# Two transformer blocks on one core: single steps between the matmul passes put together in twos

## The chip, the cores and the metric

The kernel runs on one core of one Trainium2 chip. The metric is the device time of one execution, in microseconds (us). Before the change the median of three runs is 1921.94 us (1920.91 to 1922.42).

The engines' names in the profile: PE is TensorE (its weight loads are a row of their own, PEld), DVE is VectorE, ACT is ScalarE, POOL is GpSimd, SP issues most transfers. Each engine works through its own queue in order, and semaphores hold an instruction until what it needs is there.

## The reference, cut to what matters

Two blocks follow each other on x of 512 tokens by 1024. In the first: a modulated norm, stick-breaking attention of 16 heads, a retention of 4 heads, gates, an output projection and an FFN. In the second: an attention over chosen keys of 8 heads, a gated linear attention, a projection and an FFN.

```python
# block 1
proj = einsum('bsd,de->bse', hmix, w_in[l])
z = einsum('bhtd,bhsd->bhts', qb, kb) * scale            # stick breaking, block of 128 queries
log_1m_beta = where(mask, log_sigmoid(-z), 0.0)
after = cumsum(log_1m_beta, axis=3, reverse=True) - log_1m_beta
a = where(mask, exp(log_sigmoid(z) + after), 0.0)
outs.append(einsum('bhts,bhsd->bhtd', a, vb))
...
scores = einsum('bhncd,bhnmd->bhncm', qc, kc) * decay_mask   # retention
intra = einsum('bhncm,bhnme->bhnce', scores, vc)
...
x = x + gate1 * einsum('bsd,de->bse', merged, w_out[l])
...
# block 2
logits = einsum('bqhd,bqkhd->bqhk', qb, kg) * A_HEAD_DIM ** -0.5 + bias
p = softmax(where(valid, logits, NEG), axis=-1)
o_a = einsum('bqhk,bqkhd->bqhd', p, vg)
...
return rmsnorm_2(x, norm_final)
```

## The kernel before

Nearly all of TensorE's time goes to large products. Each weight tile is split into a high and a low part (`wh`, `wl`: ACT copies the high part from `stg`, POOL or DVE subtracts to get the low part), each activation likewise, and one **pass step** of a job is three matmuls of 128x128 weights with 512 columns: high by high, low by high, high by low (L1465, L1466, L1468). Eight such steps make one job, one output tile of 128 features by 512 tokens. POOL's subtraction for a weight tile is L2559.

Between pass steps stands the other work of PE: products in plain fp32 and transposes. It comes from Python generators. A planner writes one list of steps, in which every engine finds its own in that order. After each pass step `slot` adds the stage's rate to a credit and advances the first generator in `p.fore` by one `yield` for each whole credit. So a `yield` in a generator is a place where pass steps may come in between, `rest(m)` is m of them, and what two yields enclose stands on PE with nothing between. `p.later` holds steps that are emitted after a following job. `take` and `give` hand out the eight PSUM banks from rings: G (three banks, the jobs), Z and C (two each), O (one). `take` only decides the order; that a bank has been emptied is waited for on the chip (`free`).

The generators that the change touches:

- `attend(pr)`, one for each of eight pairs of heads, at rate 1.3. Scores come in three groups (`sbz`, L1511); DVE adds the mask (L1808); ACT takes two sigmoids (`sba`, L2261 and L2263); DVE runs the product scan over one and multiplies the other with it (`sbr`, L1819 and L1823), which gives five tiles of weights `zs`; PE turns each by four 128x128 transposes (`sbt`, L1495 `bank<-ident,zs`); ACT copies the turned tile out (`sbe`, L2269); `sbo` (L1531) multiplies with the values.
- `v_after(pr)`: the values of a pair are turned (`sbvt`, L1495) one job after their product is done.
- `retain(hh)`: three score products (`rs`, L1547) and four products with the values (`rvv`, L1561), one to a yield.
- `out_job(f)`: the turn of an x tile (`x2t`, L1588) stands ahead of each output job.
- `attn()`: 16 items (pair, block of queries). Item n has its logits (`al`, L1689, 64 rows of the array for each of two heads), the maximum (`ag`), the exponential (`ae`), the division (`as`, L2112), the turned weights (`at`, L1697), their copies by ACT (`ac`, L2492) and the values (`av`, L1710, 64 columns of the array for each of two heads). Logits of item n, turns of item n-2 and values of item n-3 stand in three different slots of an iteration.
- `turn_x()`: the final turns of x (`xo`, L1495 `bank<-ident,XR`), one in every eight slots.

Of the kernel before, what the change touches and what calls it, by code (L numbers as in the profile page):

```python
# [16 lines left out]
KT = D // P  # L17
# [232 lines left out]
def make_plan():  # L250
    p = Plan()
# [109 lines left out]
    def attend(pr):  # L361
        if pr == 0:
            emit("tables", "sb")

        def scores(g):
            for hh in range(2):
                take("Z", ("sbz", pr, g, hh))
            emit("sbz", pr, g)
            for hh in range(2):
                give(("sbz", pr, g, hh))  # L370

        def turned(n):
            take("C", ("sbt", pr, n))
            emit("sbt", pr, n)
            yield
            emit("sbe", pr, n)
            give(("sbt", pr, n))

        scores(0)
        yield from rest(3)  # L380
        emit("sba", pr, 1)
        yield from rest(2)
        emit("sba", pr, 2)
        scores(1)
        yield from rest(2)
        emit("sbr", pr, 1)
        yield from rest(2)
        emit("sba", pr, 0)
        yield
        emit("sbr", pr, 2)  # L390
        yield
        scores(2)
        yield from turned(1)
        yield
        emit("sbr", pr, 0)
        emit("sba", pr, 3)
        yield from rest(2)
        yield from turned(2)
        yield
        emit("sba", pr, 4)  # L400
        yield
        emit("sbr", pr, 3)
        yield from turned(0)
        yield from rest(2)
        emit("sbr", pr, 4)
        yield from rest(2)
        yield from turned(3)
        yield from rest(3)
        yield from turned(4)
        yield from rest(2)  # L410
        while ("v", pr) not in p.known:
            yield
        take("O", ("sbo", pr))
        emit("sbo", pr)
        yield
        yield
        p.split("os", pr, "pool")
        emit("sbw", pr)
        give(("sbo", pr))
        yield  # L420

    def v_after(pr):
        def turn():
            take("G", ("sbvt", pr))
            emit("sbvt", pr)
            give(("sbvt", pr))
            p.known.add(("v", pr))
        p.later.append([1, turn])
        p.fore.append(attend(pr))

    for p2 in range(1, 4):
# [50 lines left out]
        emit("factor", key)  # L482

    def retain(hh):
        for n in range(3):
            take("Z", ("rs", hh, n))
            emit("rs", hh, n)
            give(("rs", hh, n))
            yield
        while ("rv", hh, 3) not in p.known:  # L490
            yield
        for d in range(4):
            take("C", ("rvv", hh, d))
            emit("rvv", hh, d)
            give(("rvv", hh, d))
            yield
        yield
        yield
        take("O", ("r", hh))
# [99 lines left out]

    def out_job(f):  # L600
        def fn(n):
            take("Z", ("x2t", f))
            emit("x2t", f)
            give(("x2t", f))
            take("G", ("gemm", n, 0), 0)
            p.gemm(n)
            p.of["out", f] = n
# [342 lines left out]
    def attn():  # L950
# [31 lines left out]
        for n in range(len(ITEMS) + 3):  # L982
            if wanted(n, 0):
                logits(n)
            if wanted(n, 1):
                emit("ae", n - 1)
            yield
# [13 lines left out]
            if n < 3:  # L1001
                yield
                yield
            if wanted(n, 3):
                while ("VA", ITEMS[n - 3][0]) not in p.known:
                    yield
                values(n - 3)
            if wanted(n, 1):
                emit("as", n - 1)
            yield  # L1010
# [47 lines left out]
    def turn_x():  # L1058
# [4 lines left out]
        factor("n4")  # L1063
        give("n4")
        p.known.add("r4")
        for k in range(KT):
            for _ in range(8):
                yield
            take("Z", ("xo", k))
            emit("xo", k)  # L1070
            give(("xo", k))

    def norm4():
        p.mark("last")
# [1614 lines left out]
```

## Time and profile before

| | us |
|---|---|
| median of 3 runs | 1921.94 |
| lowest, highest | 1920.91, 1922.42 |
| the profiled execution | 1923.94 |
| its span, first to last instruction | 1922.1 |
| PE busy in the span | 1879.3 |
| DVE, ACT, POOL busy | 868.0, 687.2, 516.4 |

The profiled execution lies 2.0 us above the median of the runs, and 1.8 us of it lie outside the span. Matmuls are pipelined: a row's length reaches into the next one, so a cost on PE is read from the starts of rows. A bracket at the end of a row gives the idle time ahead of it and who ended it.

### The profile page before, as it was taken

What the parts mean: (1) busy time and instruction counts of PE and PEld (TensorE: products, weight loads), DVE (VectorE), ACT (ScalarE), POOL (GpSimd) and SP (SyncE); (2) the same over time, 40 slices, a digit from 0 to 9 for tenths busy, and PEclk for the clock granted to TensorE, in tenths of its full rate; (3) what the DMA queues carried; (4) which work ended last, traced back from release to release, by engine and by line L of the source; (5) the groups of instructions that cost most, each with busy time, mean ns of one, the idle gap of its engine ahead of it and who ended that gap; (6) DMA issues with size and microseconds to landing.
All of it is one profiled execution on the core that took longest, in us unless ns stands there. A gap on an engine that the chain in (4) does not pass through costs nothing.

```text
span 1922.1 us, 21539 instructions
## 1 busy us (share of the span) xinstructions
PE 1879.3 (98%) x8653; PEld 1463.2 (76%) x8653; DVE 868.0 (45%) x1352; ACT 687.2 (36%) x1021; POOL 516.4 (27%) x285
## 2 busy tenths in 40 slices
PE   7999999999999999989999999999999999999998
PEld 6777778878777777867888888777676778888886
DVE  6466542645261213334333333657477654423433
ACT  5555541223232323443221223425446432212223
POOL 4433334444353534410000000234345311100100
PEclk9999999999999999999999999999899999999999
DMA  9411223534443223324323322422122123222321
GB/s 302 144 46 65 66 66 132 175 121 153 132 141 100 66 88 110 102 74 118 114 82 95 108 80 77 113 88 84 58 72 73 46 99 104 93 88 89 108 88 44
DMA packets 182332, 192.47 MB, mean 100 GB/s; under 512 B 10155, under 2 KB 166065, under 8 KB 181977
## 3 DMA queue, kind: packets, MB, share of 16 engines
q1 hardware_dynamic: 179704, 180.84, 29.3%
q0 software_dynamic: 1104, 5.24, 1.0%
q10 hardware_dynamic: 1424, 5.00, 0.7%
q8 instruction: 70, 1.15, 0.3%
q14 instruction: 30, 0.24, 0.0%
HBM read 188.95 MB, written 4.72 MB: 101 GB/s over the span
## 4 chain that ended last, share of the span: by engine, by line
PE 87%; DVE 8%; ACT 2%; issue 2%; POOL 1%; DMA 0%; ACTq 0%; DVEq 0%; SPq 0%; POOLq 0%
PE bank L1465 23%; PE bank L1468 23%; PE bank L1466 23%; PE bank L1487 2%; PE bank L1486 2%; PE bank L1485 2%; PE bank L1561 2%; DVE left L1819 2%; PE bank L1495 1%; DVE ADA L1777 1%; PE bank L1531 1%; PE bank L1547 1%; PE bank L1511 1%; PE bank L1447 1%; PE bank L1448 1%
## 5 line engine op out<-in xcount | busy, mean ns | idle before, releaser
L2559 POOL TENSOR_TENSOR wl<-stg,wh 128x1024 fp32r<-128x1024 f32 x150 | 364.8, 2433 | 853.5 <-ACT wh L2200 853.1
L1465 PE MATMUL bank<-hH,wh 128*128 128x512 f32 x1264 | 522.6, 413 | 6.3 <-DVE hL L1933 6.0
L1468 PE MATMUL bank<-hH,wl 128*128 128x512 f32 x1264 | 502.4, 397 | 0.0
L1466 PE MATMUL bank<-hL,wh 128*128 128x512 f32 x1264 | 502.1, 397 | 0.0
L2200 ACT ACTIVATE wh<-stg 128x1024 fp32r<-128x1024 f32 (+2 forms) x292 | 298.3, 1024 | 283.6 <-PE bank L1468 202.8
L1465 PEld LDWEIGHTS bank<-hH,wh 128*128 128x128 f32 x1264 | 239.2, 189 | 78.4 <-issue 25.5
L1468 PEld LDWEIGHTS bank<-hH,wl 128*128 128x128 f32 x1264 | 238.9, 189 | 57.9
L1466 PEld LDWEIGHTS bank<-hL,wh 128*128 128x128 f32 x1264 | 239.8, 190 | 53.5 <-issue 2.9
L1759 DVE TENSOR_TENSOR wl<-stg,wh 128x1024 fp32r<-128x1024 f32 (+2 forms) x142 | 168.4, 1188 | 243.7 <-ACT wh L2200 243.2
L1465 PE MATMUL bank<-h2H,wh 128*128 128x512 f32 x352 | 140.6, 399 | 0.0
L1468 PE MATMUL bank<-h2H,wl 128*128 128x512 f32 x352 | 139.5, 396 | 0.0
L1466 PE MATMUL bank<-h2L,wh 128*128 128x512 f32 x352 | 139.5, 396 | 0.0
L2607 POOL TENSOR_TENSOR tmp<-tmp,SQ 128x512 f32<-128x512 f32 x22 | 28.5, 1294 | 295.6 <-ACT tmp L2388 295.6
L1777 DVE SCALAR_TENSOR_TENSOR ADA<-stg,small,ADA 128x256 f32<-128x256 f32 x112 | 88.7, 792 | 3.7
L1468 PEld LDWEIGHTS bank<-h2H,wl 128*128 128x128 f32 x352 | 66.3, 188 | 16.1
L1466 PEld LDWEIGHTS bank<-h2L,wh 128*128 128x128 f32 x352 | 66.3, 188 | 16.0 <-issue 0.2
L1465 PEld LDWEIGHTS bank<-h2H,wh 128*128 128x128 f32 x352 | 66.3, 188 | 16.0 <-issue 0.2
L1950 DVE TENSOR_TENSOR tmp<-bank,tmp 128x512 f32<-128x512 f32 x44 | 30.4, 692 | 91.6 <-PE bank L1468 91.5
L1468 PE MATMUL bank<-fHa,wl 128*128 128x512 f32 x176 | 69.8, 396 | 0.0
L1465 PE MATMUL bank<-fHa,wh 128*128 128x512 f32 x176 | 69.8, 396 | 0.0
L1466 PE MATMUL bank<-fLa,wh 128*128 128x512 f32 x176 | 69.8, 396 | 0.0
L1819 DVE TENSOR_TENSOR_SCAN left<-tmp,masks 128x384 f32<-128x384 f32 (+2 forms) x64 | 61.9, 999 | 0.0
(324 smaller groups left out, 2565.3 us busy)
## 6 DMA issues: line engine op xcount, KB each, us to landing
stg<-in_w_in SPq DMA_DIRECT2D x54, 1024.0 KB, 5.2
stg<-in_w_ffn_in SPq DMA_DIRECT2D x22, 1024.0 KB, 5.1
stg<-in_w_ada SPq DMA_DIRECT2D x16, 1024.0 KB, 5.2
stg<-in_w_ffn_gate SPq DMA_DIRECT2D x11, 1024.0 KB, 5.1
stg<-in_w_ffn_up SPq DMA_DIRECT2D x11, 1024.0 KB, 5.1
stg<-in_w_ffn_down SPq DMA_DIRECT2D x10, 1024.0 KB, 5.0
stg<-in_w_ada SPq DMA_DIRECT2D x16, 512.0 KB, 6.8
stg<-in_w_proj_ret SPq DMA_DIRECT2D x8, 1024.0 KB, 5.0
```

The costliest lines, as they stand in the source:

```text
L1465: T.matmul(ps, wh, xh, start=j["first"] and k == 0, stop=False)
L1466: T.matmul(ps, wh, xl, start=False, stop=False)
L1468: t = T.matmul(ps, wl, xh, start=False, stop=j["stop"] and last)
L1485: T.matmul(gb[:, :], xh, wh, start=s0, stop=False)
L1486: T.matmul(gb[:, :], xh, wl, start=False, stop=False)
L1487: t = T.matmul(gb[:, :], xl, wh, start=False, stop=s1)
L1561: t = T.matmul(cb[:, j * P:S], v[:, j, d * P:(d + 1) * P], TMP[4 + n][:, off:off + w], start=j == 0, stop=j == 3)
L1759: V.tensor_tensor(lo, src, hi, ALU.subtract).then_inc(s["w_lo_dve"], 1)
L1777: V.scalar_tensor_tensor(last, view[:, k, :], cact[:, k:k + 1], acc, ALU.mult, ALU.add).then_inc(s["ada"], 1)
L1819: t = V.tensor_tensor_scan(left[:, back], tt[:, back], masks[:, 3, back], 1.0, ALU.mult, ALU.add)
L2200: A_.activation(hi, src, ACTF.Copy).then_inc(s["w_hi"], 1)
L2559: G.tensor_tensor(lo, src, hi, ALU.subtract).then_inc(s["w_lo_pool"], 1)
```

## The change

Steps that stood alone between pass steps stand together: the turned weights of the first attention as (1, 2), (0, 3) and (4); the turned values of two pairs; the retention's scores as (0, 1) and (2), its products with the values as (0, 1) and (2, 3); two turns of x ahead of every second output job; two final turns of x after sixteen slots. In the second attention the values of item n-3 move from the third slot of an iteration into the first, behind the logits of item n. Sizes, buffers and the arithmetic stay.

```diff
-        def turned(n):
-            take("C", ("sbt", pr, n))
-            emit("sbt", pr, n)
-            yield
-            emit("sbe", pr, n)
-            give(("sbt", pr, n))
+        def turn(*ns):
+            for n in ns:
+                take("C", ("sbt", pr, n))
+                emit("sbt", pr, n)
+
+        def turned(*ns):
+            for n in ns:
+                emit("sbe", pr, n)
+                give(("sbt", pr, n))
...
         scores(2)
-        yield from turned(1)
+        yield from rest(2)
+        turn(1, 2)
         yield
+        turned(1, 2)
         emit("sbr", pr, 0)
+        yield from rest(2)
         emit("sba", pr, 3)
         yield from rest(2)
-        yield from turned(2)
-        yield
         emit("sba", pr, 4)
         yield
         emit("sbr", pr, 3)
-        yield from turned(0)
-        yield from rest(2)
+        yield from rest(3)
+        turn(0, 3)
+        yield
+        turned(0, 3)
         emit("sbr", pr, 4)
-        yield from rest(2)
-        yield from turned(3)
         yield from rest(3)
-        yield from turned(4)
+        turn(4)
+        yield
+        turned(4)
...
         def turn():
-            take("G", ("sbvt", pr))
-            emit("sbvt", pr)
-            give(("sbvt", pr))
-            p.known.add(("v", pr))
-        p.later.append([1, turn])
+            for q in (pr - 1, pr):
+                take("G", ("sbvt", q))
+                emit("sbvt", q)
+            for q in (pr - 1, pr):
+                give(("sbvt", q))
+                p.known.add(("v", q))
+        if pr % 2:
+            p.later.append([1, turn])
...
-        for n in range(3):
-            take("Z", ("rs", hh, n))
-            emit("rs", hh, n)
-            give(("rs", hh, n))
-            yield
+        for lot in ((0, 1), (2,)):
+            for n in lot:
+                take("Z", ("rs", hh, n))
+                emit("rs", hh, n)
+            for n in lot:
+                give(("rs", hh, n))
+                yield
...
-            take("Z", ("x2t", f))
-            emit("x2t", f)
-            give(("x2t", f))
+            if f % 2 == 0:
+                for g in (f, f + 1):
+                    take("Z", ("x2t", g))
+                    emit("x2t", g)
+                    give(("x2t", g))
...
             if wanted(n, 0):
                 logits(n)
+            if wanted(n, 3):
+                while ("VA", ITEMS[n - 3][0]) not in p.known:
+                    yield
+                values(n - 3)
             if wanted(n, 1):
                 emit("ae", n - 1)
...
-            if wanted(n, 3):
-                while ("VA", ITEMS[n - 3][0]) not in p.known:
-                    yield
-                values(n - 3)
...
-        for k in range(KT):
-            for _ in range(8):
-                yield
-            take("Z", ("xo", k))
-            emit("xo", k)
-            give(("xo", k))
+        for k in range(0, KT, 2):
+            yield from rest(16)
+            for g in (k, k + 1):
+                take("Z", ("xo", g))
+                emit("xo", g)
+                give(("xo", g))
```

The products `rvv` are put together like `rs`, in `((0, 1), (2, 3))`. Lines of the changed file lie 15 lower from L1103 on (L1465 is L1480 there).

PE in the second attention, before: logits of one item (`KA,QA`), then turned weights (`ident,lg`, 8 transposes), then values (`tmp,VA`), a pass step between each:

```order
L1689 MATMUL bank<-KA,QA 128x256 x2
L1465 MATMUL bank<-goH,wh 128x512
L1466 MATMUL bank<-goL,wh 128x512
L1468 MATMUL bank<-goH,wl 128x512
L1697 MATMUL bank<-ident,lg 128x128 x8
L1465 MATMUL bank<-goH,wh 128x512
L1466 MATMUL bank<-goL,wh 128x512
L1468 MATMUL bank<-goH,wl 128x512
L1710 MATMUL bank<-tmp,VA 64x128 x6
```

The same item now:

```order
L1704 MATMUL bank<-KA,QA 128x256 x2
L1725 MATMUL bank<-tmp,VA 64x128 x6
L1480 MATMUL bank<-goH,wh 128x512
L1481 MATMUL bank<-goL,wh 128x512
L1483 MATMUL bank<-goH,wl 128x512
L1712 MATMUL bank<-ident,lg 128x128 x8
```

The values have come up behind the logits, and no pass step stands between the two; the turned weights keep a pass step on either side.

PE in the first attention, third pair of heads, before: the third group of scores (`k2,q2`) and the first turn (`zs1`); four pass steps follow before `zs2`:

```order
L1511 MATMUL bank4<-k2,q2 128x512
L1511 MATMUL bank3<-k2,q2 128x512
L1495 MATMUL bank5<-ident,zs1 128x128 x4
L1465 MATMUL bank1<-hH,wh0 128x512
L1466 MATMUL bank1<-hL,wh0 128x512
L1468 MATMUL bank1<-hH,wl0 128x512
```

The same place now:

```order
L1526 MATMUL bank4<-k2,q2 128x512
L1526 MATMUL bank3<-k2,q2 128x512
L1480 MATMUL bank1<-hH,wh0 128x512
L1481 MATMUL bank1<-hL,wh0 128x512
L1483 MATMUL bank1<-hH,wl0 128x512
L1510 MATMUL bank5<-ident,zs1 128x128 x4
L1510 MATMUL bank6<-ident,zs2 128x128 x4
```

One pass step now parts the scores from the turns (two in some pairs), and the turn of `zs2` has moved up by three pass steps.

ACT in the same pair, before: sigmoids (L2261, L2263) and copies of turned weights (`at1`, `at2`):

```order
L2269 ACTIVATE at1<-bank5 128x512
L2261 ACTIVATE tmp1<-zs3 128x512
L2263 ACTIVATE zs3<-zs3 128x512
L2269 ACTIVATE at2<-bank6 128x512
L2238 ACTIVATE q2<-bank1 128x512
```

ACT there now:

```order
L2284 ACTIVATE at1<-bank5 128x512
L2284 ACTIVATE at2<-bank6 128x512
L2276 ACTIVATE tmp1<-zs3 128x512
L2278 ACTIVATE zs3<-zs3 128x512
L2276 ACTIVATE tmp2<-zs4 128x512
```

The copy of `at2`, which waits for the turn of `zs2`, now stands ahead of the sigmoids of `zs3`.

## Rows read from the trace of the kernel before

**Rows 1.** The page: busy time of each engine, share of the span, instructions.
```profile
PE 1879.3 (98%) x8653; PEld 1463.2 (76%) x8653; DVE 868.0 (45%) x1352; ACT 687.2 (36%) x1021; POOL 516.4 (27%) x285
```

**Rows 2.** Waits of PE: who waited for whom; total, times, longest.
```profile
PE bank L1495 <- DVE zs L1823: 5.0, 8, 1.0
PE bank L1672 <- DVE tmp L2077: 2.1, 1, 2.1
```

**Rows 3.** Timeline of PE, unbroken passes: start, length, what.
```profile
299.70 0.40 PE L1465 MATMUL bank<-osH,wh 128*128 128x512 f32 x1
...
311.89 0.40 PE L1466 MATMUL bank<-osL,wh 128*128 128x512 f32 x1
```

**Rows 4.** Timeline of PE, one turn of weights between passes.
```profile
217.05 0.39 PE L1468 MATMUL bank<-hH,wl 128*128 128x512 f32 x1
217.29 0.60 PE L1495 MATMUL bank<-ident,zs 128*128 128x128 f32 x4
...
218.42 0.39 PE L1465 MATMUL bank<-hH,wh 128*128 128x512 f32 x1
```

**Rows 5.** Timeline of PE, second attention: values, logits, turned weights, values.
```profile
1487.13 0.40 PE L1468 MATMUL bank<-goH,wl 128*128 128x512 f32 x1
1487.46 0.66 PE L1710 MATMUL bank<-tmp,VA 128*64 128x128 f32 x8
...
1488.61 0.40 PE L1468 MATMUL bank<-goH,wl 128*128 128x512 f32 x1
...
1489.57 0.50 PE L1465 MATMUL bank<-goH,wh 128*128 128x512 f32 x1
1489.91 0.39 PE L1466 MATMUL bank<-goL,wh 128*128 128x512 f32 x1
1490.14 0.39 PE L1468 MATMUL bank<-goH,wl 128*128 128x512 f32 x1
1490.37 0.60 PE L1697 MATMUL bank<-ident,lg 128*128 128x128 f32 x4
1490.81 0.60 PE L1697 MATMUL bank<-ident,KI 128*128 128x128 f32 x4
...
1491.71 0.40 PE L1468 MATMUL bank<-goH,wl 128*128 128x512 f32 x1
1492.04 0.88 PE L1710 MATMUL bank<-tmp,VA 128*64 128x128 f32 x12
...
1493.41 0.40 PE L1468 MATMUL bank<-goH,wl 128*128 128x512 f32 x1
```

**Rows 6.** Timeline of PE, third group of scores: third pair, then sixth pair.
```profile
125.29 1.13 PE L1511 MATMUL bank<-k,q 64*128 64x512 f32 x4
...
208.13 1.13 PE L1511 MATMUL bank<-k,q 64*128 64x512 f32 x4
```

**Rows 7.** Timeline of DVE, third pair: products giving zs2 and zs3.
```profile
128.56 0.69 DVE L1823 TENSOR_TENSOR zs<-zs,left 128x511 f32<-128x511 f32 x1
...
133.52 2.88 DVE L1823 TENSOR_TENSOR zs<-zs,left 128x511 f32<-128x511 f32 x1
```

**Rows 8.** Timeline of POOL there: the low part of a weight tile.
```profile
133.44 2.40 POOL L2559 TENSOR_TENSOR wl<-stg,wh 128x1024 fp32r<-128x1024 f32 x1 [7.97 <-ACT wh L2200]
```

**Rows 9.** Timeline of DVE, sixth pair: products giving zs2 and zs3.
```profile
208.41 0.69 DVE L1823 TENSOR_TENSOR zs<-zs,left 128x511 f32<-128x511 f32 x1
...
214.59 0.69 DVE L1823 TENSOR_TENSOR zs<-zs,left 128x511 f32<-128x511 f32 x1
```

**Rows 10.** Timeline of PE, second attention: turn of the first values.
```profile
1442.25 0.66 PE L1495 MATMUL bank<-ident,tmp 128*128 128x128 f32 x4
```

**Rows 11.** Timeline of ACT there: copies of those values.
```profile
1442.94 1.14 ACT L2422 ACTIVATE VA<-bank,small 128x128 f32<-128x128 f32 x4 [0.53 <-PE bank L1495]
```

**Rows 12.** Stretches: length, busy PE, PEld, DVE, ACT, POOL, PEclk, DMA share, GB/s.
```profile
60.00:280.00 220.00, 214.96 (x1264) 160.41 (x1263) 133.54 (x168) 118.15 (x183) 77.57 (x35) 1.00 0.20 64
...
1356.00:1370.00 14.00, 14.00 (x40) 9.50 (x40) 2.89 (x3) 4.88 (x7) 0.84 (x1) 0.52 0.24 76
```

More of the change, by code:

```diff
@@ L484, in retain @@
     def retain(hh):
-        for n in range(3):
-            take("Z", ("rs", hh, n))
-            emit("rs", hh, n)
-            give(("rs", hh, n))
-            yield
+        for lot in ((0, 1), (2,)):
[5 more added lines that the diff above has]
+                yield
         while ("rv", hh, 3) not in p.known:
             yield
[L492 to L495, printed above, removed]
-            yield
+        for lot in ((0, 1), (2, 3)):
+            for d in lot:
+                take("C", ("rvv", hh, d))
+                emit("rvv", hh, d)
+            for d in lot:
+                give(("rvv", hh, d))
+                yield
         yield
@@ L984, in attn @@
                 logits(n)
+            if wanted(n, 3):
+                while ("VA", ITEMS[n - 3][0]) not in p.known:
+                    yield
+                values(n - 3)
             if wanted(n, 1):
@@ L1065, in turn_x @@
         p.known.add("r4")
-        for k in range(KT):
-            for _ in range(8):
-                yield
-            take("Z", ("xo", k))
-            emit("xo", k)
-            give(("xo", k))
+        for k in range(0, KT, 2):
[4 more added lines that the diff above has]
+                give(("xo", g))
     def norm4():
```

## The prediction, made before the changed kernel ran

> **What bounds the kernel now.** I read the busy times first: PE is busy for 98% of the span [rows 1], so time can only go where PE waits or where its rows follow each other more slowly than they must. Then the waits of PE: the largest that this change touches is that of the turned weights for DVE's products, 5.0 us in 8 waits, the longest 1.0 [rows 2]. Then the timeline of PE, from start to start, since lengths overlap. Unbroken passes: 52 steps between the two rows of [rows 3], 12.19 us, so 0.234 us a matmul. Any step between passes is then priced by the distance between passes around it, less 0.234 for each pass matmul in it.
>
> **What joining saves on PE.** One turn of weights: 217.05 to 218.42 is 1.37, four pass matmuls are 0.94, so it costs 0.43 [rows 4]. Eight transposes in one go: 1490.14 to 1491.71 is 1.57, less three passes 0.70, so 0.87 [rows 5]. That is twice 0.43: a turn pays nothing for standing alone, and putting two together saves nothing. The turns of x and of the values are the same four transposes of 128 by 128. The retention's scores and products also use all 128 rows and columns of the array, as passes and turns do; I take nothing for them too, from the nearest rows, with a bound of 0.1 either way for each of their 12 joins, 1.2 us in all.
>
> Logits and values of the second attention are another thing. Values of 8 records: 1487.13 to 1488.61 is 1.48, less 0.70, so 0.78; of 12 records: 1491.71 to 1493.41 is 1.70, less 0.70, so 1.00 [rows 5]. Four records are 0.22, so 0.34 of each group is a fixed price. It is seen at the edges: the values start 0.33 after the pass ahead of them and not 0.23 (1487.13 to 1487.46), and the first pass behind the logits is followed after 0.34 and not 0.23 (1489.57 to 1489.91). Put together, the pass between logits and values goes, and with it the slow step behind the logits (0.11) and the slow start of the values (0.10): 0.21 a join. The values of items 1 to 12 are joined so (those of item 0 have to wait for a turn of VA and stand alone, those of the last three have no logits beside them): 12 joins, 2.5 us saved. The bounds: nothing, if values behind logits pay both steps as they do behind a pass; 12 x 0.34 = 4.1, if the values' fixed price goes altogether. I take 2.5, which is what the rows show at the two edges that go.
>
> The Trainium skill says (TensorEngine Tiling (Array Packing), section Tiling Modes, Key Properties) that "Changing tiling mode (not just tile) drains the TensorE". The rows bear it out: only the steps on part of the array have slow edges. Logits take 64 rows and values 64 columns, so by this rule one change of mode stays between them, which gives 2.5 and not 4.1.
>
> One join is undone: the first turn stood right behind the third scores and is now parted from them by one or two pass steps. The scores' slow step is then paid before a pass; at most 0.11 for each of 8 pairs. I take half: +0.4.
>
> **What waits.** The first attention decides the rest. DVE's product is 0.69 us, but 2.88 where it begins beside POOL's subtraction of a weight tile (133.52, inside 133.44 to 135.84) [rows 7, 8]. So a pair's five products come early or late by up to 2.2 us. The Trainium skill has this as a lock (SBUF — State Buffer, section Who interferes with whom): of two instructions that need the shared ports, the one that began first keeps them to its end. The two rows agree.
>
> Now the dates. Scores begin at 125.29 in the third pair and 208.13 in the sixth [rows 6]. The tile zs2 is done 3.96 later (128.56 + 0.69) in the third and 0.97 later in the sixth; zs3 11.11 later (133.52 + 2.88) and 7.15 later [rows 7, 9]. In the changed order the turn of zs2 comes after the scores (1.13), three passes (0.70) and the turn of zs1 (0.43): 2.26 after the scores began. Then the turn, 21 pass matmuls (4.92) and the turn of zs0: zs3 is wanted 5.78 after zs2 began. Third pair: a wait of 1.70, then 3.96 + 5.78 = 9.74 against 11.11, another 1.37; 3.1 together. Sixth pair: none in either place. zs0, which most of today's eight waits are for, is now wanted four slots later and is safe; zs4 keeps its distance of nine pass matmuls from the turns ahead.
>
> I count two quiet pairs of eight and give the other six half of the late one: 6 x 1.55 = 9.3. Today the eight waits cost 5.0 idle, and about 0.25 each for the refilling of the array that no bracket counts (an estimate from the slow edges above), 7.0 in all. So +2.3. Bounds: all waits gone, -7.0; all six as late as the third, 18.6 - 7.0 = +11.6. Also ACT now copies at2 ahead of the sigmoids of zs3. These are wanted by DVE only after the product of zs0, which takes longer than the copy, so I cost this at nothing; if a pass's copy and a weight tile get in front as well, it is part of the +11.6.
>
> The turned values go in pairs, so two of the three banks of ring G are taken between jobs and the next job waits for ACT to empty the third. Two turns are 0.87, and a copy of 512 columns takes at most the 1.14 of four copies of 128 [rows 11]: 0.3 in each of three places at most, and I take nothing.
>
> In the second attention the first values now come one pass step after the turn of VA. That turn begins at 1442.25, takes 0.43, and three passes 0.70: 1443.4; ACT's copies end at 1444.08 (1442.94 + 1.14) [rows 10, 11]. A new wait of 0.7. Later items have 1.4 us of passes and the logits between a turned weight and its values, which covers two copies; I cost them at nothing, with 2 us as the bound if ACT stands in a weight tile's copy. What is queued behind a waiting PE row is everything: all of these are on the path.
>
> **The sum.** -2.5 + 0.4 + 2.3 + 0.7 = +0.9 us. Against the profiled execution's own 1923.94, that is 1924.8; it lies 2.0 above the median of the runs, so 1922.8 against 1921.94. A change of under 0.2% (3.8 us) cannot be told from none here; this is one.
>
> **The rivals.**
>
> 1. A stretch at half clock goes away: faster. From 1356 to 1370 the granted clock is 0.52 of full, the level of 1.2 GHz and not 2.4 [rows 12], right after PE had waited 2.1 us for one product of DVE [rows 2]. Waits of up to 1.0 in the first attention brought no fall: the clock there is 1.00 [rows 12]. So a wait near 2 us can, and perhaps need not, cost a fall. No instruction near that place is moved, but all of it shifts by the microseconds won or lost before. If it falls away, up to 14 x 0.48 = 6.7 us come back: 1922.8 - 6.7 = 1916. Against it: the wait itself stays as it is, and three runs lie within 1.5 us, so the fall seems to come each time. Chance 0.20.
> 2. The turned weights wait less instead of more: faster. With zs0 wanted later, the waits go and zs2 is rarely late: 1921.94 - 7.0 - 2.5 + 1.1 = 1913.5. For it: two of eight pairs are quiet. Against it: zs2 loses two passes' distance in every pair. Half of it would be 1917. Chance 0.08.
> 3. The turned weights pile up: slower. In four of eight pairs or more POOL's subtraction meets a product of zs2 or zs3, as in the third pair; 6 x 3.1 - 7.0 = +11.6 at most, and +5 to +8 where four or five meet; 1927 to 1930. It decides from the point where zs2 is over 3 us behind the scores in most pairs. A wait near 2 us at one of them may also bring the half clock, which adds some 3 (half the price of rival 1). Chance 0.17.
> 4. Each step that stands alone pays a fixed price, as the values do: 12 joins of values, 16 of weights, 12 of the retention, and 11 of turns of x and of values would give 51 x 0.34 = 17 us, 1905. The eight transposes at 0.87 speak against it. Chance 0.03.
>
> **How the numbers follow.** No measurable change has 0.52; its own range is 1918.5 to 1925.5. Faster by over 0.2%: rivals 1, 2 and 4, of the first a little falls short (0.17 + 0.08 + 0.03), and 0.02 from the likeliest, 0.30. Slower: rival 3 and a little of the likeliest, 0.18. The range takes in rival 1 at the lower end and the first part of rival 3 at the upper: 1915 to 1927.5; rivals 2 and 4 and the late half of 3 are left out.
>
> **What would show it.** Right: the values follow the logits at once, and the distance around both falls by 0.2 against the two apart; turns of 8 cost 0.87; the wait of L1495 (then L1510) for DVE moves from zs0 to zs2 and zs3 and stands at 5 to 9 us; a wait near 0.7 stands ahead of the first values. Wrong: waits under 4 us or over 12; a clock row near 1356 to 1370 that is 1.00; turns in twos cheaper than 0.87.

## The result and the profile after

Measured: 1932.26 us median of the changed kernel (1931.38 to 1934.58) against 1921.81 of the kernel before beside it (1920.91 to 1922.42): ratio 1.0056, 95% interval 1.0044 to 1.0069. It is slower by 10.5 us, on the side of rival 3 and above the 1927 to 1930 named there; the forecast was 1922.8, in a range of 1915 to 1927.5, and no measurable change.

Lines below L1103 have moved down by 15: the passes are now L1480, L1481 and L1483, the turns L1510, the third scores L1526, DVE's scan and product L1834 and L1838.

PE, ACT and POOL are busy for as long as in [rows 1], within 1 us; PE does the same work in a span longer by 7.5 us. DVE is busy for 11.6 us more with the same 1352 instructions:

```profile
PE 1878.8 (97%) x8653; PEld 1466.2 (76%) x8653; DVE 879.6 (46%) x1352; ACT 686.4 (36%) x1021; POOL 515.7 (27%) x285
```

The waits of PE (who waited for whom; total, times, longest) answer to [rows 2]:

```profile
PE bank L1510 <- DVE zs L1838: 11.7, 14, 2.0
...
PE bank L1687 <- DVE tmp L2092: 2.1, 1, 2.1
PE bank L1712 <- DVE lg L2127: 2.0, 2, 1.2
...
PE bank L1725 <- ACT VA L2437: 0.5, 1, 0.5
```

The turned weights wait 11.7 us in 14 waits where they waited 5.0 in 8; the waits for the division of the second attention (`lg`) are 2.0 where they were 1.2; the wait for the first values (`VA`) is new.

Where in the program the time goes is seen best by laying the passes of the two traces side by side: both have the same 6912 pass matmuls in the same order, so how much later each starts shows where time is lost.

| stretch, by the clock of before | later by the end of it than at its start, us |
|---|---|
| start to 24.6 (no moved step yet) | +0.6 |
| 24.6 to 302, first attention | +10.5 |
| 302 to 1352, retention, output, turns of x, FFN | +0.1 |
| 1352 to 1413, the half-clock stretch | -3.2 |
| 1413 to 1533, second attention | -0.55 |
| 1533 to the end, final turns of x | 0.0 |
| sum | +7.5 |

The stretches (us, busy PE, PEld, DVE, ACT, POOL, granted clock, DMA share, GB/s) answer to [rows 12]:

```profile
60.00:220.00 160.00, 151.49 (x868) 111.80 (x867) 104.98 (x124) 84.79 (x133) 53.34 (x24) 1.00 0.20 64
220.50:223.50 3.00, 3.00 (x9) 2.22 (x8) 0.70 (x2) 0.23 (x1) 0.00 (x0) 0.50 0.55 187
1367.50:1374.00 6.50, 6.50 (x24) 5.23 (x22) 1.07 (x1) 1.23 (x2) 0.52 (x1) 0.50 0.52 161
1374.50:1381.00 6.50, 6.50 (x28) 3.98 (x24) 1.50 (x2) 3.66 (x5) 0.00 (x0) 1.00 0.01 3
```

The old stretch at 1.2 GHz behind the 2.1 us wait is there, but it is 6.8 us long and not 13.7; a new one of 3.4 us stands at 220, in the first attention, and takes 1.7 us. The old one has either length in traces of kernels that differ only far from it, and the change is not shown to be the cause (see the part left open). Without its 3.2, the two traces differ by 10.7, close to the 10.5 of the medians.

**Inside the first attention.** The sixth pair, timeline of PE (start, length, what, idle time ahead), from the third scores on:

```profile
208.27 1.13 PE L1526 MATMUL bank<-k,q 64*128 64x512 f32 x4
...
210.14 0.60 PE L1510 MATMUL bank<-ident,zs 128*128 128x128 f32 x4
211.45 0.66 PE L1510 MATMUL bank<-ident,zs 128*128 128x128 f32 x4 [0.72 <-DVE zs L1838]
...
216.86 0.60 PE L1510 MATMUL bank<-ident,zs 128*128 128x128 f32 x4
219.43 0.66 PE L1510 MATMUL bank<-ident,zs 128*128 128x128 f32 x4 [1.97 <-DVE zs L1838]
```

The second turn of each pair of turns waits: zs2 behind zs1 by 0.7, zs3 behind zs0 by 2.0. ACT in the same stretch:

```profile
210.77 0.60 ACT L2284 ACTIVATE at<-bank 128x512 f32<-128x512 f32 x1 [3.92 <-PE bank L1510]
212.14 0.60 ACT L2284 ACTIVATE at<-bank 128x512 f32<-128x512 f32 x1 [0.78 <-PE bank L1510]
213.55 0.60 ACT L2266 ACTIVATE tmp<-bank 128x512 f32<-128x512 f32 x1 [0.81 <-PE bank L1483]
214.04 1.05 ACT L2215 ACTIVATE wh<-stg 128x1024 fp32r<-128x1024 f32 x1
214.99 0.62 ACT L2276 ACTIVATE tmp<-zs 128x512 f32<-128x512 f32 x1
215.64 0.63 ACT L2278 ACTIVATE zs<-zs 128x512 f32<-128x512 f32 x1
```

The copy of at2 waits for the late turn of zs2; a pass's copy (which again waits for PE) and a weight tile's high part follow; only then, at 214.99, 6.7 after the scores, the sigmoids of zs3. In the sixth pair of the kernel before they came 2.25 after the scores, which began at 208.13 [rows 6]:

```profile
210.38 0.62 ACT L2261 ACTIVATE tmp<-zs 128x512 f32<-128x512 f32 x1
```

In the changed kernel the high part at 214.04 has also released POOL's subtraction for the same tile, which lies where DVE now comes to zs3:

```profile
215.17 2.40 POOL L2574 TENSOR_TENSOR wl<-stg,wh 128x1024 fp32r<-128x1024 f32 x1 [6.69 <-ACT wh L2215]
```

DVE there, answering to [rows 9]: the product of zs0, then the scan and product of zs3, then the scan of zs4:

```profile
213.81 0.69 DVE L1838 TENSOR_TENSOR zs<-zs,left 128x511 f32<-128x511 f32 x1
215.65 3.01 DVE L1834 TENSOR_TENSOR_SCAN left<-tmp,masks 128x512 f32<-128x512 f32 x1 [1.15 <-ACT tmp L2276]
218.69 0.69 DVE L1838 TENSOR_TENSOR zs<-zs,left 128x511 f32<-128x511 f32 x1
219.30 1.22 DVE L1834 TENSOR_TENSOR_SCAN left<-tmp,masks 128x512 f32<-128x512 f32 x1
```

DVE idles 1.15 for the sigmoids, and the scan then takes 3.01, beside the subtraction, where the next one, of the same shape, takes 1.22. The seventh and eighth pairs look alike (scans of 3.0).

Over the eight pairs DVE's scans and products are held up beside such a subtraction once in each half of each pair, 16 times, and in the kernel before 12 times. They take 30.5 us more than undisturbed ones (scans of 1.22 for 512 columns down to 0.40 for 128, products of 0.69) where they took 22.4 more before: that is 8.1 of the 11.6 by which DVE's busy time grew.

For all eight pairs: the distance from the row ahead of a turn to the turn, less the undisturbed distance (0.23 behind a pass, 0.52 behind scores, 0.11 behind another turn), summed by tile in each trace, with those of five experiments that follow below. This holds the idle time of the bracket and some 0.16 more at each wait, which no bracket counts.

| us, eight pairs | zs1 | zs2 | zs0 | zs3 | zs4 | sum | first attention, passes later by |
|---|---|---|---|---|---|---|---|
| before | 1.0 | 0.2 | 3.9 | 1.3 | 0.0 | 6.4 | 0 |
| after | 0.0 | 5.4 | 0.0 | 6.8 | 2.2 | 14.4 | +10.5 |
| sigmoids first | 0.0 | 5.4 | 0.0 | 0.0 | 4.2 | 9.6 | +4.4 |
| zs1, zs2 later | 0.0 | 0.2 | 1.5 | 6.2 | 5.1 | 12.9 | +7.6 |
| both | 0.0 | 0.2 | 1.5 | 4.4 | 6.3 | 12.3 | +7.0 |
| in twos, old dates | 0.0 | 0.2 | 0.0 | 1.1 | 2.8 | 4.1 | -1.7 |
| one by one, zs0 late | 0.6 | 0.2 | 0.0 | 2.0 | 2.3 | 5.2 | -1.0 |

After less before is 8.0; with 1.7 for the half clock and 0.4 for the scores parted from the turn it is 10.1 of the 10.5 (0.2 of the zs4 column is the half clock counted again).

### The profile page after: what moved, and what is told of

Same layout as the page of the kernel before. It is cut to its first block, busy times and chain, and to the rows that moved or that the text cites. A ratio compares the mean times of both kernels' runs of the same rounds, so it can differ in the third digit from the quotient of the medians.

```text
span 1929.6 us, 21521 instructions
## 1 busy us (share of the span) xinstructions
PE 1878.8 (97%) x8653; PEld 1466.2 (76%) x8653; DVE 879.6 (46%) x1352; ACT 686.4 (36%) x1021; POOL 515.7 (27%) x285
## 3 DMA queue, kind: packets, MB, share of 16 engines
q8 instruction: 70, 1.15, 0.3%
## 4 chain that ended last, share of the span: by engine, by line
PE 85%; DVE 10%; ACT 3%; issue 2%; POOL 1%; DMA 0%; ACTq 0%; DVEq 0%; SPq 0%; POOLq 0%
PE bank L1480 23%; PE bank L1483 22%; PE bank L1481 22%; DVE left L1834 3%; PE bank L1502 2%; PE bank L1500 2%; PE bank L1501 2%; PE bank L1576 2%; DVE ADA L1792 1%; PE bank L1510 1%; PE bank L1546 1%; PE bank L1562 1%; DVE zs L1838 1%; PE bank L1526 1%; PE bank L1462 1%
## 5 line engine op out<-in xcount | busy, mean ns | idle before, releaser
L1480 PE MATMUL bank<-hH,wh 128*128 128x512 f32 x1264 | 519.5, 411 | 6.3 <-DVE hL L1948 6.0
L1483 PE MATMUL bank<-hH,wl 128*128 128x512 f32 x1264 | 502.9, 398 | 0.0
L1481 PE MATMUL bank<-hL,wh 128*128 128x512 f32 x1264 | 502.5, 398 | 0.0
L1480 PEld LDWEIGHTS bank<-hH,wh 128*128 128x128 f32 x1264 | 239.2, 189 | 82.2 <-issue 28.0
L1483 PEld LDWEIGHTS bank<-hH,wl 128*128 128x128 f32 x1264 | 239.1, 189 | 58.1
L1481 PEld LDWEIGHTS bank<-hL,wh 128*128 128x128 f32 x1264 | 239.8, 190 | 53.6 <-issue 1.9
L1480 PE MATMUL bank<-h2H,wh 128*128 128x512 f32 x352 | 140.3, 399 | 0.0
L1483 PE MATMUL bank<-h2H,wl 128*128 128x512 f32 x352 | 139.5, 396 | 0.0
L1481 PE MATMUL bank<-h2L,wh 128*128 128x512 f32 x352 | 139.5, 396 | 0.0
L1481 PEld LDWEIGHTS bank<-h2L,wh 128*128 128x128 f32 x352 | 66.3, 188 | 16.2 <-issue 0.2
L1483 PEld LDWEIGHTS bank<-h2H,wl 128*128 128x128 f32 x352 | 66.3, 188 | 16.2
L1480 PEld LDWEIGHTS bank<-h2H,wh 128*128 128x128 f32 x352 | 66.3, 188 | 16.2 <-issue 0.2
L1834 DVE TENSOR_TENSOR_SCAN left<-tmp,masks 128x384 f32<-128x384 f32 (+2 forms) x64 | 72.3, 1159 | 2.3 <-ACT tmp L2276 2.3
L1483 PE MATMUL bank<-fHa,wl 128*128 128x512 f32 x176 | 69.8, 396 | 0.0
L1480 PE MATMUL bank<-fHa,wh 128*128 128x512 f32 x176 | 69.8, 396 | 0.0
L1481 PE MATMUL bank<-fLa,wh 128*128 128x512 f32 x176 | 69.8, 396 | 0.0
```

The lines of the kernel that those rows point to most:

```text
L1480: T.matmul(ps, wh, xh, start=j["first"] and k == 0, stop=False)
L1481: T.matmul(ps, wh, xl, start=False, stop=False)
L1483: t = T.matmul(ps, wl, xh, start=False, stop=j["stop"] and last)
L1834: t = V.tensor_tensor_scan(left[:, back], tt[:, back], masks[:, 3, back], 1.0, ALU.mult, ALU.add)
```

## The experiments

Line numbers differ by a few from kernel to kernel; the names tell what a row is. Theory 1: all of the loss is the turned weights of the first attention. Under it, theory A: ACT's order makes zs3 late; theory B: the dates alone, turns asked for before DVE can have them. Theory J, the rival to all: putting turns together costs something of itself.

**All but the weights.** The five turns as in the kernel before, one by one; everything else changed.

```diff
-        yield from rest(2)
-        turn(1, 2)
+        yield from turned(1)
...
-        turn(0, 3)
+        yield from turned(0)
```

> The changed kernel with the first attention's turns of weights put back one by one as in the kernel before; all other joins stay. In the two traces the passes of the changed kernel run 11.1 us later than those of the kernel before once the first attention is done, gain 0.5 in the second attention and differ by 0.1 elsewhere, but for a half-clock stretch near 1370 that is 6.8 us long in one trace and 13.7 in the other. Theory 1 (all of the loss is the turned weights): 1921.8 - 0.5 = 1921.3, PE's waits for the products of zs back at about 5 us in 8. Theory 2 (the values' turns in pairs, which also lie in the first attention, or ring G, carry a part): between 1924 and 1930. If the shorter half-clock stretch comes with the new order of the second half, some 3 us less by either.

Measured 1920.91 (1920.2 to 1922.97) against 1922.28: ratio 0.9993, interval 0.9984 to 1.0002. In the trace the first attention differs from before by -0.2, the second by -0.56, the rest but for the half-clock stretch by 0.5. So the turned values in pairs, the retention and the turns of x cost or give no more than 0.5, and theory 1 stands.

**The weights only.** The other way round: the kernel before, with only the new order of the five turns.

```diff
-        yield from turned(1)
+        yield from rest(2)
+        turn(1, 2)
...
-        yield from turned(0)
+        turn(0, 3)
```

> The kernel before with only the first attention's turns of weights put in twos. Theory 1: 1921.8 + 11.1 = 1932.9, waits of PE for the products of zs near 11.7 us in 14, with one or two near 2 us and perhaps a half-clock stretch behind one of them. Theory 2 (the loss needs the turned values in pairs beside it): 1924 to 1928. If the second attention's joins really gave 0.5, this kernel is 0.5 slower than the changed one.

Measured 1935.11 (1930.57 to 1936.31): ratio 1.0063, interval 1.0049 to 1.0077. First attention +11.3, second 0.0, waits for zs 12.5 in 14, and again a half-clock stretch of 3.4 us at 221 behind a wait of 2.0. Theory 1 again; the median is 2.2 above the 1932.9 expected.

**Sigmoids first.** The changed kernel, with the sigmoids of zs3 ahead of the two copies.

```diff
+        emit("sba", pr, 3)
         turned(1, 2)
         emit("sbr", pr, 0)
         yield from rest(2)
-        emit("sba", pr, 3)
```

> The changed kernel with one row of ACT's order moved: the sigmoids of zs3 stand ahead of the copies of the turned at1 and at2, not behind them. Theory A (ACT's line: at2's copy waits for a late turn, a pass's copy and a weight tile get in front, and zs3 comes late): the four waits of turn 3 in the last four pairs (gaps of 1.24, 2.24, 1.64 and 2.14 us against 0.11) go, 6.8 us, and with them the half-clock stretch at 220 (1.7): 1932.3 - 8.5 = 1923.8; the waits for zs2 stay (0.7 to 1.2 in seven pairs). Theory B (the dates alone: zs2 and zs3 are asked for before DVE can have them, whatever ACT does): the waits of turn 3 stay, 1930 to 1933. Theory C (POOL's subtraction decides where DVE is slow): the waits move to other pairs, 1928 to 1932.

Measured 1926.93 (1926.08 to 1929.6): ratio 1.0026, interval 1.0016 to 1.0037; 5.3 less than the changed kernel's median, from another set of runs, and 6.1 less in the first attention by the passes. The waits of PE:

```profile
PE bank L1510 <- DVE zs L1838: 7.1, 14, 1.2
```

The sixth pair, ACT, then PE, then DVE:

```profile
212.26 0.63 ACT L2276 ACTIVATE tmp<-zs 128x512 f32<-128x512 f32 x1 [5.18 <-DVE zs L1823]
212.93 0.63 ACT L2278 ACTIVATE zs<-zs 128x512 f32<-128x512 f32 x1
213.46 1.07 ACT L2284 ACTIVATE at<-bank 128x512 f32<-128x512 f32 x2
```

```profile
217.09 1.03 PE L1510 MATMUL bank<-ident,zs 128*128 128x128 f32 x8
...
220.70 0.66 PE L1510 MATMUL bank<-ident,zs 128*128 128x128 f32 x4 [0.47 <-DVE zs L1838]
```

```profile
216.52 3.40 DVE L1834 TENSOR_TENSOR_SCAN left<-tmp,masks 128x512 f32<-128x512 f32 x1
219.96 0.69 DVE L1838 TENSOR_TENSOR zs<-zs,left 128x511 f32<-128x511 f32 x1
```

The eight transposes of zs0 and zs3 now stand as one row: no wait for zs3 in any pair, and no half clock at 220. Theory A holds for the 6.8 us and the 1.7 behind them, in part by way of theory C: in the fifth pair DVE had not waited for ACT, but POOL's subtraction, released by ACT, had begun 0.23 ahead of the product of zs3 and now begins 0.14 behind it. I had expected 8.5 back and got some 6: the slow scan has gone to zs4 (3.40), whose turn waits 4.2 where it waited 2.2.

**Turns of zs1 and zs2 later**, by two slots; zs3's sigmoids stay behind the copies.

```diff
         scores(2)
-        yield from rest(2)
+        yield from rest(3)
+        emit("sbr", pr, 0)
+        yield
         turn(1, 2)
         yield
         turned(1, 2)
-        emit("sbr", pr, 0)
-        yield from rest(2)
         emit("sba", pr, 3)
```

> The changed kernel with the turn of zs1 and zs2 two slots later (about 1.1 us) and everything behind it in its slot; on ACT zs3's sigmoids still stand right behind the copies of at1 and at2. Theory B (dates): the waits for zs2, 0.55 to 1.35 us in seven pairs, 5.5 in all with what refills the array behind each, go; the waits for zs3 shrink too, since zs2's turn, its copy and the sigmoids are no later than now: 1932.3 - 7 = 1925, or less. Theory A: only the zs2 waits go, those of zs3 stay at 1 to 2 us in the last four pairs: 1932.3 - 5.5 = 1926.8, the half-clock stretch near 220 still there. If neither, the turns are late because of what DVE does ahead of them and the time stays at 1931 or more.

Measured 1929.94 (1928.91 to 1931.62): ratio 1.0043, interval 1.0030 to 1.0055. The waits for zs2 go as both theories had it (5.4 to 0.2), those of zs3 stay near the size that A had (6.8 to 6.2), though mostly not for A's reason, as the next run shows. Neither had that zs4 rises from 2.2 to 5.1, and the time is 3 us above A's 1926.8. The longest wait is 1.7, and there is no half clock in the first attention.

**Both edits.**

> Both edits of the two runs before put together: the turn of zs1 and zs2 two slots later, and zs3's sigmoids ahead of the copies of at1 and at2. Theory L (a chain of fixed length: from the third scores through the mask, the sigmoids, the scans and products to zs4 takes DVE and ACT 12.1 to 12.6 us, and the last turn is asked for before that): the waits of zs2 and zs3 go, and what they cost comes back as a wait of zs4 of 1.2 to 1.5 us in each pair, 8 x 1.3 = 10 against the 9.6 that zs2 and zs4 cost with the sigmoids alone moved (1926.9): 1926 to 1928. Theory S (each wait has its own cause and goes with it): zs4 waits as with the sigmoids alone (4.2 in all), 1926.9 - 5.4 = 1921.5.

Measured 1928.8 (1927.73 to 1930.27): ratio 1.0034, interval 1.0021 to 1.0046, 0.8 above the range of theory L and far from the 1921.5 of theory S; by the passes the first attention is 2.6 longer than with the sigmoids alone. zs4 waits 1.15 to 1.5 in five pairs, as theory L had it; in the other three it is zs3 (1.0 to 1.4) and not zs4, so L's account of each pair was too neat. These three waits for zs3 (1.37, 1.04, 1.37) are the same to 0.01 with the sigmoids behind the copies, in the run before; only the wait of the fifth pair (1.86) goes. So with the later turns it is not ACT's order that makes zs3 late there: in both runs POOL's subtraction lies beside a scan or product of zs0 or zs3. The length of the chain is not fixed either: the product of zs4 ends 11.6 to 13.0 us after the third scores in the changed kernel and in the last three runs, 8.8 to 13.0 in the kernel before. What holds is that PE asks for the last turn before DVE is through, and part of what it does not wait for earlier it waits for there.

**In twos at the old dates.** Each pair of turns in the slot of the later of the two before; sigmoids of zs3 in slot 2 as before.

```diff
         scores(2)
         yield from rest(2)
+        emit("sbr", pr, 0)
+        emit("sba", pr, 3)
+        yield from rest(2)
         turn(1, 2)
         yield
         turned(1, 2)
-        emit("sbr", pr, 0)
-        yield from rest(2)
-        emit("sba", pr, 3)
-        yield from rest(2)
+        yield
...
+        emit("sbr", pr, 4)
+        yield from rest(2)
         turn(0, 3)
         yield
         turned(0, 3)
-        emit("sbr", pr, 4)
```

> The changed kernel with its turns still in twos, but each pair of turns in the slot where the later of the two stood before: zs1 and zs2 in slot 4, zs0 and zs3 in 12, zs4 in 16, values in 19; zs3's sigmoids stand in slot 2 as before. Theory L (dates alone): no turn is asked for earlier than before and the one that waited (zs0) five slots later; of the 4.5 us of idle time in 8 waits that the kernel with all but the weights changed has (1920.9), 1 to 1.5 are left, and 0.25 for the refilling goes with each wait that goes: 1920.9 - 3.3 - 1.5 + 0.4 (scores parted) = 1916.5. Theory J (putting two turns together costs something itself, by the two banks of ring C that are held at once or the copies that come in twos): 1921 or more.

Measured 1921.58 (1919.07 to 1922.56) against 1922.17: ratio 0.9994, interval 0.9984 to 1.0003. The waits of PE:

```profile
PE bank L1511 <- DVE zs L1839: 3.1, 5, 1.0
```

The first attention is 1.7 us shorter than before and 12.2 shorter than in the changed kernel, with the same eight transposes in one go. By the median alone, theory J's 1921 or more has come true and theory L's 1916.5 has not; it is the passes that speak against J, for with all joins kept the first attention is shorter than with none. So the joins cost nothing, and the loss lay in the dates and in ACT's order, which this run changes together: the sigmoids of zs3 stand ahead of the copies again. The gain was smaller than I had expected (1.7, not 4.4), since zs4 again takes over part of the waits (2.8), and the half-clock stretch has its long form (13.7) in this trace.

**One by one, zs0 late.** For comparison, single turns with zs0's moved three slots back.

> The changed kernel with the turns of weights one by one as before, but zs0's turn three slots later (behind the scan and product of zs4 in the plan). Theory L: the five waits for zs0 (0.5 to 1.2 us each, 3.9 us together in the kernel before) go, those of zs1 and zs3 in the third and fourth pair (1.0, 0.7, 0.6) stay or grow by 0.5: 1920.9 - 3.4 - 1 = 1916.5. If the waits only move to zs3 and zs4, 1919 to 1921. Against the same dates with turns in twos: equal, if eight transposes in a go save nothing (0.87 for 2 x 0.43).

Measured 1922.27 (1920.61 to 1924.11): ratio 1.0001, interval 0.9992 to 1.001. First attention -1.0: the waits for zs0 are gone as expected, those of zs3 and zs4 have taken most of them, as in the second of the two cases named, though the time lies above the 1919 to 1921 given for it. In twos it is 0.7 better by the passes, most of it the wait for zs1 (0.6), whose turn comes later there.

**The same, with the ends of the second attention apart**: values join logits except those of item 0 and of the last three.

```diff
-            if wanted(n, 3):
+            if wanted(n, 3) and wanted(n, 0) and n > 3:
...
+            if wanted(n, 3) and not (wanted(n, 0) and n > 3):
+                while ("VA", ITEMS[n - 3][0]) not in p.known:
+                    yield
+                values(n - 3)
```

> The same as the run before, and in the second attention the values that have no joined logits to gain from stand where they did: those of item 0, which now wait 0.7 us for the copies of VA, and those of the last three items, ahead of which a turn waits 1.2 us (0.8 before) for DVE's lg. Theory: 0.7 and up to 1.65 come back (the passes there lose 1.65 between the last logits and the last turns but one): 1916.5 - 2 = 1914.5. Rival: the late wait for lg comes from POOL's subtraction beside three of DVE's rows there (1.38, 1.18 and 2.17 us instead of 0.35 to 0.42), which the place of the values doesn't change: 1916.

Measured 1917.89 (1917.03 to 1920.47): ratio 0.9978, interval 0.9969 to 0.9986, faster than both kernels, though not the 1914.5 expected, which was reckoned from 1916.5 for the run before. The second attention gives 2.91 by the passes where the changed kernel gives 0.55: 2.4 come back, as the theory had it, and the wait for `VA` is gone. The rival had the cause of the late `lg` right (POOL's subtraction beside the division) but not that it would stay: the division of 384 columns that took 2.17 is undisturbed here. Between the traces of this run and the one before, another 3.0 us are the half-clock stretch, 6.8 long here and 13.7 there.

**In twos at the old dates, ends apart.**

> The turns of weights in twos at their old dates, and in the second attention the values of item 0 and of the last three items where they stood before. The traces so far: the first gives 1.5 us of passes against turns one by one at the dates of the kernel before, the second 2.4. Theory D (the two add, as they lie a millisecond apart): 1921.6 - 2.4 = 1919.2, or 1917.1 as 0.8 below the run with zs0 late and the ends apart (1917.9). Rival: the gain of the second attention was the length of the half-clock stretch near 1370 alone (6.8 us there against 13.7), so no more than 0.5 against the same weights with all values joined.

Measured 1919.93 (1916.67 to 1920.63) against 1922.29: ratio 0.9984, interval 0.9975 to 0.9992. The waits:

```profile
PE bank L1515 <- DVE zs L1843: 3.1, 5, 1.0
...
PE bank L1717 <- DVE lg L2132: 0.8, 1, 0.8
```

First attention -1.7, second -2.91: the two gains add, and the second is there with a half-clock stretch of 13.7 as well, so it is not made of it. The second wait for `lg` has gone.

**The same, with no values joined.**

> The same with the second attention wholly as in the kernel before: no values behind logits. Theory D: the 11 joins of logits and values that the run before keeps gave 0.21 each by the slow edges, 2.3 to 2.9 in all, so this one is 2.3 to 2.9 slower than the run before it: about 1919.9. Rival (joined values save nothing, the passes only stand elsewhere): no difference, 1917.

Measured 1922.19 (1919.65 to 1923.12): ratio 0.9997, interval 0.9988 to 1.0006. Second attention 0.0 against -2.91: by the passes, the joins give 2.9 us. They are 12 (items 1 to 12), not 11 as I wrote, so 0.24 each. The medians differ by 2.3.

## Why the prediction was wrong

**The step that failed** is the one on ACT: "ACT now copies at2 ahead of the sigmoids of zs3. These are wanted by DVE only after the product of zs0, which takes longer than the copy, so I cost this at nothing". I priced the copy's length, not its wait. The copy waits for a turn that itself waits for DVE, and two other rows of ACT come in behind it, so the sigmoids come 1.5 to 4.5 us later in the last three pairs than in the kernel before, and the slow scan comes with them. Measured: 6.8 us of waits for zs3 in four pairs (5.7 in these three; in the fifth, 1.1, DVE does not wait for ACT, but the product lies beside POOL's subtraction and takes 2.7), against 4.1 in my count for zs3 (6 x half of 1.37); and 1.7 us of half clock behind the wait of 2.0, which the sum did not have and rival 3 named at some 3. Moving that one row of ACT gave 5 to 6 us of the 10.5 back. I had even written down what happens, as the case "if a pass's copy and a weight tile get in front as well", and put it in a bound rather than asking whether it must.

**"I count two quiet pairs of eight"** failed too. Not one pair is quiet: in each, POOL's subtraction meets a scan of zs1 or zs2 (1.9 to 3.2 us instead of 0.4 or 1.0), in the kernel before in five of eight. The sixth pair, which I had read as quiet: DVE's two scans for zs1 in the kernel before, then in the changed one, with POOL's subtraction.

```profile
205.20 1.26 DVE L1819 TENSOR_TENSOR_SCAN left<-tmp,masks 128x384 f32<-128x384 f32 x2
```

```profile
205.34 3.42 DVE L1834 TENSOR_TENSOR_SCAN left<-tmp,masks 128x384 f32<-128x384 f32 x2
205.75 2.73 POOL L2574 TENSOR_TENSOR wl<-stg,wh 128x1024 fp32r<-128x1024 f32 x1 [4.61 <-ACT wh L2215]
```

I read this so: quiet was not a property of the pair but of the date at which a weight tile was due, and the change moved the pairs against the tiles. With turns in twos at the old dates these scans of pairs 5 to 7 are undisturbed again; no run took the subtraction off POOL to show it directly. That the size for zs2 came out, 5.4 against 6 x 0.85 = 5.1, is luck: there were seven waits of 0.2 to 1.3, from slow scans, where the count had six of one size.

**zs4** "keeps its distance of nine pass matmuls from the turns ahead" was read as no cost. It waits 2.2, nearly all of it in the first four pairs (0.45 to 0.62 each): there POOL's subtraction lies beside zs4's product (2.71 instead of 0.69) or its scan. First pair, DVE and POOL:

```profile
81.55 2.71 DVE L1838 TENSOR_TENSOR zs<-zs,left 128x511 f32<-128x511 f32 x1
81.31 2.40 POOL L2574 TENSOR_TENSOR wl<-stg,wh 128x1024 fp32r<-128x1024 f32 x1 [7.74 <-ACT wh L2215]
```

In the kernel before, zs4's product was as slow in two pairs, and its turn did not wait, for PE had waited for zs0 ahead of it.

So the term of the waits, +2.3, was +8.0 (zs2 5.4, zs3 6.8, zs4 2.2, less 6.4 of today's waits, which I had put at 7.0), and with the half clock +9.7; its own bound of +11.6 held it, but the range ended at the first part of rival 3. Rival 3 had the right sign and the first link (POOL beside DVE); it missed the scans, which were hit more often than the products, and ACT's queue. Rival 2, that the waits shrink, did not come.

The Trainium skill has the lock as an exclusive one for two-input operations (SBUF — State Buffer, section Who interferes with whom). The scan agrees: it began 0.48 after the subtraction, which had 1.92 left, and took 1.79 longer than the next scan, as the product of [rows 7] did beside [rows 8].

**What was right.** Eight transposes in a go cost twice four, 0.87 or 0.88: 107.67 to 109.25 is 1.58, less three passes 0.70 [rows 4, 5]:

```profile
107.67 0.39 PE L1483 MATMUL bank<-hH,wl 128*128 128x512 f32 x1
107.91 1.03 PE L1510 MATMUL bank<-ident,zs 128*128 128x128 f32 x8
108.70 0.47 PE L1480 MATMUL bank<-hH,wh 128*128 128x512 f32 x1
109.01 0.40 PE L1481 MATMUL bank<-hL,wh 128*128 128x512 f32 x1
109.25 0.40 PE L1483 MATMUL bank<-hH,wl 128*128 128x512 f32 x1
```

Rival 4 falls with it. One reading of mine was too strong: not only steps on part of the array have a slow edge. The first pass behind these transposes, too, is followed after 0.31 and not 0.23; but since eight cost twice four, that edge is no price for standing alone. The retention's joins came to nothing (0.1 us over 1050). The scores parted from the turn cost 0.05 in each pair, 0.4, as taken. The new wait for the first values: 0.73 by the passes, against the 0.7 worked out from [rows 10, 11]:

```profile
1452.10 0.44 PE L1725 MATMUL bank<-tmp,VA 128*64 128x128 f32 x4 [0.53 <-ACT VA L2437]
```

And the joins of logits and values: 0.24 each, against 0.21 and a bound of 0.34. Timeline of PE at one of them, to be set against the values alone of [rows 5]:

```profile
1491.70 0.40 PE L1483 MATMUL bank<-goH,wl 128*128 128x512 f32 x1
1492.02 0.49 PE L1704 MATMUL bank<-KA,QA 64*128 64x128 f32 x4
1492.44 0.66 PE L1725 MATMUL bank<-tmp,VA 128*64 128x128 f32 x8
1493.03 0.50 PE L1480 MATMUL bank<-goH,wh 128*128 128x512 f32 x1
1493.37 0.39 PE L1481 MATMUL bank<-goL,wh 128*128 128x512 f32 x1
```

The values stand right behind the logits; one slow start (0.32) and one slow step at the end (0.34) are left of two each.

**A term that was not there.** The second attention gave 0.55 and not 2.5 - 0.7 = 1.8, because near its end a turn waits for the division, which lies beside POOL's subtraction of a weight tile and takes 2.17 where 384 columns took 0.42 in the kernel before (PE, DVE, POOL):

```profile
1512.62 0.55 PE L1712 MATMUL bank<-ident,lg 128*128 128x128 f32 x3 [1.24 <-DVE lg L2127]
1510.39 2.17 DVE L2127 TENSOR_SCALAR lg<-lg,small 128x384 f32<-128x384 f32 x1
1509.98 2.37 POOL L2574 TENSOR_TENSOR wl<-stg,wh 128x1024 fp32r<-128x1024 f32 x1 [2.11 <-ACT wh L2215]
```

There the passes lose some 1.6. With the values of the ends where they stood, this wait and that for `VA` go together, and the joins' 2.9 stay. Which of the two places removed it was not tried apart.

**Left open.** What sets the length of the stretch near 1360: it is 6.8 us in some traces and 13.7 in others, worth 3.2 us by the passes. Of twelve traces it is short in the changed kernel, in all but the weights, in the weights only, the sigmoids first, the later turns, both edits and zs0 late with the ends apart, long in the others and in the kernel before. It seems to go with the execution and not with the kernel: the five traces with the long form have a mean granted clock of 0.993, the seven with the short one 0.994 or 0.995, and of 65 executions of the kernel before, beside the experiments, 19 had 0.993 and took 1923.7 to 1924.8 us, the other 46 had 0.994 or 0.995 and took 1920.8 to 1923.0. The traced execution of the kernel before, from which I reckoned, was one of the longer kind. Rival 1, that the stretch goes away, did not come in any trace: it comes each time, as I had thought, but not at one length.

## What to carry to other kernels

When a step of one engine is moved up, look at what its follower is queued ahead of on the next engine: a copy of 0.6 us that waits for a late producer holds everything behind it for as long as the producer is late. Price the wait and the rows that slip in behind it, and ask what those rows release in turn. And removing one wait of a chain shows only what the next one asks for: here part of the time moved from zs3, or from zs2, to zs4, and only the old dates and the old order on ACT together gave it back.

## What the runs showed that I had not expected

A wait of PE of 1.97 us, the longest in the first attention, was followed within 1 us by 3.4 us at a granted clock of 0.50, in both kernels that had such a wait there. In the same two kernels the wait of 1.87 in the eighth pair was followed by no fall, and neither was the longest wait, 1.7, of the kernel with the later turns.

DVE's scan, not only its product, is held beside POOL's subtraction: 3.0 to 3.4 us instead of 1.22 for 512 columns; and so is the division of the second attention, 2.17 instead of 0.42 for 384.

The passes repeat to 0.1 us between kernels in stretches that are alike: the second attention gave -0.55, -0.56, -0.49, -0.51, -0.51, -0.51 and -0.53 in the seven kernels with the changed order there and -2.91 in both with the ends apart. Differences that the times of whole runs (spread 2 to 4 us) can't resolve are plain there.
